# Forming the recurrent row's decays, key directions and deviations in PSUM banks: a two-block transformer kernel on one core

## The reference, cut to what matters

```
w_log = -softplus(-(w0 + tanh(w_low) @ w2)) - 0.5
decay = exp(-exp(w_log))                      # = exp(-exp(-0.5) * sigmoid(w0 + ...))
a = sigmoid(a0 + a_low @ a2)
g = sigmoid(g_low) @ g2
k_mod = k * (1.0 + (a - 1.0) * k_a)
kk = heads(k * k_k)
kk = kk / maximum(sqrt(sum(kk * kk, axis=-1)), 1e-12)
# scan over the positions t, 16 heads of 64 x 64 state
sa = state @ (-kk)
state = state * decay + sa * (kk * a) + v * k_mod
y = state @ r
# behind the scan, for each head
y = (y - mean) * rsqrt(var + 64e-5) * lnx_w + lnx_b
out = (y + sum(r * k_mod * r_k) * v) * g
```

## Time and profile before

| what | value |
|---|---|
| median of 3 runs | 2094.07 us (2093.38 to 2094.23) |
| the profiled execution's own time | 2093.18 us |
| its span | 2091.4 us |
| PE busy | 2035.6 us (97%) |
| PE weight loads busy | 1680.5 us (80%) |
| DVE busy | 1196.7 us (57%) |
| ACT busy | 535.9 us (26%) |
| POOL busy | 1107.7 us (53%) |
| mean granted clock of TensorE | 0.991 |

### The profile page before, as it was taken

One profiled execution on the slowest core, in us unless ns is written; L12 is line 12 of the kernel. 1 busy time (PEld: TensorE's weight loads), 2 busy tenths in 40 slices (PEclk: granted clock), 3 DMA queues, 4 the chain that ended last, 5 costly groups with the idle time before them and its releaser, 6 DMA issues.

```text
span 2091.4 us, 39582 instructions
## 1 busy us (share of the span) xinstructions
PE 2035.6 (97%) x16195; PEld 1680.5 (80%) x16195; DVE 1196.7 (57%) x1533; ACT 535.9 (26%) x1139; POOL 1107.7 (53%) x859
## 2 busy tenths in 40 slices
PE   8999999999999999999997999999999999999998
PEld 6888788878877788788876888888886878888886
DVE  7888724466667664302068676666673756565413
ACT  2100002233434212313142133333223023333101
POOL 6777764634534464454546044423364756666663
PEclk9999999999999999999999999999999999999999
DMA  4333232253443422212322022111213432322231
GB/s 135 101 101 101 92 99 65 90 166 121 141 147 116 136 81 81 81 61 70 115 66 82 14 66 66 36 56 46 65 63 116 140 101 81 100 96 88 92 111 55
DMA packets 181242, 190.27 MB, mean 91 GB/s; under 512 B 8526, under 2 KB 162269, under 8 KB 180829
## 3 DMA queue, kind: packets, MB, share of 16 engines
q1 hardware_dynamic: 172288, 181.81, 27.4%
q10 hardware_dynamic: 8796, 6.21, 1.0%
HBM read 179.56 MB, written 8.44 MB: 90 GB/s over the span
## 4 chain that ended last, share of the span: by engine, by line
PE 60%; DVE 4%; POOL 1%; issue 1%; DVEq 1%; POOLq 1%; ACT 0%; ACTq 0%
PE bank L907 8%; PE bank L909 8%; PE bank L908 8%; PE bank L1584 7%; PE bank L1545 3%; PE bank L1397 3%; PE bank L1413 2%; PE bank L1415 2%; PE bank L1414 2%; PE bank L1682 2%; PE bank L1319 1%; PE bank L1321 1%; PE bank L1320 1%; PE bank L1072 1%; PE bank L1286 1%
## 5 line engine op out<-in xcount | busy, mean ns | idle before, releaser
L738 POOL TENSOR_TENSOR wlo<-raws,whi 128x1024 fp32r<-128x1024 f32 (+5 forms) x312 | 677.6, 2172 | 46.6 <-issue 4.4
L736 POOL TENSOR_SCALAR whi<-raws 128x1024 fp32r<-128x1024 f32 (+5 forms) x312 | 331.9, 1064 | 306.8 <-PE bank L1074 173.0
L907 PE MATMUL bank<-hbuf,whi 128*128 128x512 f32 (+2 forms) x840 | 328.9, 392 | 0.0
L909 PE MATMUL bank<-hbuf,wlo 128*128 128x512 f32 (+2 forms) x840 | 327.7, 390 | 0.0
L908 PE MATMUL bank<-hbuf,whi 128*128 128x512 f32 (+2 forms) x776 | 302.7, 390 | 0.0
L649 POOL TENSOR_TENSOR spare<-ones 1x1 f32<-1x1 f32 x92 | 22.3, 243 | 345.2 <-PE bank L909 243.3
L907 PEld LDWEIGHTS bank<-hbuf,whi 128*128 128x128 f32 (+2 forms) x840 | 157.0, 187 | 35.1 <-POOL wlo L738 1.1
L909 PEld LDWEIGHTS bank<-hbuf,wlo 128*128 128x128 f32 (+2 forms) x840 | 157.0, 187 | 34.4
L908 PEld LDWEIGHTS bank<-hbuf,whi 128*128 128x128 f32 (+2 forms) x776 | 144.9, 187 | 31.1
L672 POOL TENSOR_SCALAR lg2L<-lg 128x128 fp32r<-128x128 f32 x8 | 2.7, 342 | 235.2 <-DMA lg<-in_g 235.2
L2667 DVE TENSOR_REDUCE nmax<-bank 128x4 f32<-128x512 f32 (+3 forms) x40 | 21.1, 550 | 145.5 <-PE bank L1294 104.2
(11 more groups left out here) (542 smaller groups left out, 4730.7 us busy)
## 6 DMA issues: line engine op xcount, KB each, us to landing
adaw<-in_w_ada SPq DMA_DIRECT2D x64, 384.0 KB, 3.9
raws<-in_w_up SPq DMA_DIRECT2D x22, 1024.0 KB, 4.9
raws<-in_w_in SPq DMA_DIRECT2D x41, 512.0 KB, 4.0
raws<-in_w_in SPq DMA_DIRECT2D x18, 1024.0 KB, 5.0
raws<-in_pool_w_in SPq DMA_DIRECT2D x16, 1024.0 KB, 5.4
raws<-in_mla_w_in SPq DMA_DIRECT2D x10, 1024.0 KB, 5.6
raws<-in_pool_w_out SPq DMA_DIRECT2D x8, 1024.0 KB, 5.0
raws<-in_mla_w_out SPq DMA_DIRECT2D x8, 1024.0 KB, 5.3
```

What stands on the lines that cost most here:

```text
L736: G.tensor_scalar(h_, r_, 1.0, 1.0, ALU.mult, ALU.mult)
L738: G.tensor_tensor(l_, r_, f32(h_), ALU.subtract).then_inc(raw_split, 1)
L907: M.matmul(dst, wh, acts[k][0], start=(first and k == 0), stop=False)
L909: mm = M.matmul(dst, wl, acts[k][0], start=False, stop=(last and k == n - 1))
```

## The change

It keeps a set of intermediates in PSUM banks in place of SBUF tiles. For pairs 1 and up the rates and their scanned sums lie in bank 5 (`decay_tiles`), for pairs 2 and up the grown decays too; the lengths, directions and scaled keys of all pairs lie in bank 3; the deviations of pairs 0 to 6 lie in bank 4 (`deviation_tile`). The tile kk and its multiplication are gone (ACT squares Kr with the column as its scale), and so is the multiplication by -exp(-0.5), which moves into the scales of the exponentials. ACT writes one more sigmoid for each of the pairs 1 to 7. `decayed_keys` keeps its eight instructions and gains three drains. The banks stay in use for longer, so PE gets other waits, and the second and third of the three started groups change places. Pair 0 keeps its decays in SBUF, and rT of pairs 0 and 1 still reads two SBUF tiles; so does L2868, which is not touched.

```diff
+        def deviation_tile(p):
+            return bank[4] if p < PAIRS - 1 else gn_dev
+        def decay_tiles(q):
+            return (lwd if q == 0 else bank[5], cc if q == 0 else bank[5], epos if q < 2 else bank[5])
...
             def lora_products(q):
...
                 else:
-                    pe.wait_ge(sem("rk.sig"), q)
+                    pe.wait_ge(sem("rk.kr"), q)
...
             def key_norms(q):
...
-                elif q >= 2:
+                else:
+                    pe.wait_ge(sem("rk.bon"), q)
+                if q >= 2:
                     pe.wait_ge(sem("gn.q"), q - 1)
...
             def chain(p):
...
                 started(2, Gak, vtok).then_inc(sem("sq.r"), 1)
-                pe.wait_ge(sem("rk.nr"), min(p + 2, PAIRS))
-                started(3, vtok, Gqk)
                 if p >= 1:
-                    pe.wait_ge(sem("gn.s"), p)
+                    pe.wait_ge(sem("rk.y"), p + 1)
                 else:
                     pe.wait_ge(sem("gt.taken"), 4)
                 started(4, kN, vtok, hi=CHUNKS - 1)
+                pe.wait_ge(sem("rk.bon"), min(p + 2, PAIRS))
+                started(3, vtok, Gqk)
                 pe.wait_ge(sem("inv.dve"), (p + 1) * TAKEN_ALL)
+                pe.wait_ge(sem("rk.kr"), min(p + 2, PAIRS))
                 pe.wait_ge(sem("rk.sig"), min(p + 2, PAIRS))
...
-                A.activation(lwd[:, :], lora_bank(q)[:, :], ACT.Sigmoid, bias=pc[:, 3:4])
+                rate = A.activation(lwd[:, :], lora_bank(q)[:, :], ACT.Sigmoid, bias=pc[:, 3:4])
+                if q:
+                    rate = A.activation(bank[5][:, :], bank[5][:, :], ACT.Sigmoid, bias=pc[:, 3:4])
+                rate.then_inc(sem("rk.rate"), 1)
...
             def key_squares(q):
-                act.wait_ge(sem("rk.kk"), q + 1)
-                A.activation(tile(sq, 0), kk[:, :], ACT.Square).then_inc(sem("rk.sq"), 1)
+                act.wait_ge(sem("rk.pc"), q + 1)
+                act.wait_ge(evac[1], fill("rkv", 1) + q + 1)
+                A.activation(tile(sq, 0), Kr[:, :], ACT.Square, scale=pcol[q % 3][:, 5:6]).then_inc(sem("rk.sq"), 1)
...
-                V.tensor_scalar(kk[:, :], Kr[:, :], pcol[q % 3][:, 5:6], None, ALU.mult).then_inc(sem("rk.kk"), 1)
...
-                V.tensor_scalar(lwd[:, :], lwd[:, :], -float(np.exp(-0.5)), None, ALU.mult)
...
+            def key_directions(q):
+                lengths = bank[3]
+                dve.wait_ge(sem("rk.nr"), q + 1)
+                V.reciprocal(lengths[:, :], lengths[:, :])
+                dve.drain()
+                V.scalar_tensor_tensor(lengths[:, :], Kr[:, :], pcol[q % 3][:, 5:6], lengths[:, :], ALU.mult, ALU.mult)
+                dve.drain()
+            def decayed_keys(q):
+                pc, par = pcol[q % 3], q % 2
+                direction = change = key = bank[3]
                 dve.wait_ge(sem("rk.sig"), q + 1)
                 dve.wait_ge(sem("rk.ex"), q + 1)
+                V.scalar_tensor_tensor(aT[par][:, :], direction[:, :], -1.0, lwd[:, :], ALU.mult, ALU.mult)
+                dve.drain()
+                V.tensor_tensor(direction[:, :], direction[:, :], cc[:, :], ALU.mult)
+                dve.drain()
+                V.tensor_tensor(bT[:, :], direction[:, :], aa[:, :], ALU.mult).then_inc(sem("rk.ab"), 1)
+                dve.drain()
+                V.tensor_scalar(change[:, :], aa[:, :], pc[:, 6:7], pc[:, 10:11], ALU.mult, ALU.add)
+                dve.drain()
+                V.tensor_tensor(key[:, :], Kr[:, :], change[:, :], ALU.mult)
+                dve.drain()
+                V.scalar_tensor_tensor(kkT[:, :], key[:, :], SCAN_SCALE, cc[:, :], ALU.mult, ALU.mult)
+                V.scalar_tensor_tensor(rT[par][:, :], Rr[:, :], SCAN_SCALE, decay_tiles(q)[2][:, :], ALU.mult, ALU.mult)\
                     .then_inc(sem("rk.kr"), 1)
                 dve.drain()
+                V.scalar_tensor_tensor(Rr[:, :], key[:, :], pc[:, 7:8], Rr[:, :], ALU.mult, ALU.mult)\
                     .then_inc(sem("rk.bon"), 1)
...
             def finished(p):
-                x, pc = gn_x, pcol[p % 3]
+                dev, pc = deviation_tile(p), pcol[p % 3]
                 dve.wait_ge(sem("gn.s"), p + 1)
-                V.reciprocal(gn_dev[:, :], gn_dev[:, :])
+                V.reciprocal(dev[:, :], dev[:, :])
                 dve.drain()
-                V.scalar_tensor_tensor(x[:, :], gn_y[:, :], pc[:, 8:9], gn_dev[:, :], ALU.mult, ALU.mult)
+                V.scalar_tensor_tensor(dev[:, :], gn_y[:, :], pc[:, 8:9], dev[:, :], ALU.mult, ALU.mult)
```

More of the change, by code:

```diff
@@ L34 @@
 SCAN_SCALE = 2.0 ** -20
+DECAY_RATE = float(np.exp(-0.5))
 KEY_MIN = 1e-12
@@ L368, in build @@
                     cc = sb("cc", [P, S], F32, st3)
-                    kk = sb("kk", [P, S], F32, st3)
+                    sb("beside_keys", [P, S], F32, st3)
                     epos = sb("epos", [P, S], F32, st3)
@@ L1530, in mix_part @@
                         pe.wait_ge(sem("gn.s"), PAIRS)
+                        pe.wait_ge(sem("rk.y"), PAIRS)
                     elif (kind, i, half) == ("r", 1, 1):
@@ L1749, in _ @@
                     if n == 3 * DT:
-                        pe.wait_ge(sem("rk.sig"), 2)
+                        pe.wait_ge(sem("rk.ex"), 2)
                     gate_part(1, n)
@@ L2167, in key_squares @@
             def key_squares(q):
-                act.wait_ge(sem("rk.kk"), q + 1)
-                A.activation(tile(sq, 0), kk[:, :], ACT.Square).then_inc(sem("rk.sq"), 1)
+                act.wait_ge(sem("rk.pc"), q + 1)
+                act.wait_ge(evac[1], fill("rkv", 1) + q + 1)
+                A.activation(tile(sq, 0), Kr[:, :], ACT.Square, scale=pcol[q % 3][:, 5:6]).then_inc(sem("rk.sq"), 1)
             def key_lengths(q):
                 act.wait_ge(sem("rk.ss"), q + 1)
-                A.activation(tile(sq, 1), bank[3][:, :], ACT.Relu, bias=key_floor)
+                A.activation(bank[3][:, :], bank[3][:, :], ACT.Relu, bias=key_floor)
@@ L2174, in key_lengths @@
                 act.drain()
-                A.activation(tile(sq, 1), tile(sq, 1), ACT.Sqrt, bias=key_rise).then_inc(sem("rk.nr"), 1)
+                A.activation(bank[3][:, :], bank[3][:, :], ACT.Sqrt, bias=key_rise).then_inc(sem("rk.nr"), 1)
             def decays(q):
+                _, sums, grown = decay_tiles(q)
                 act.wait_ge(sem("rk.lp"), q + 1)
-                A.activation(epos[:, :], cc[:, :], ACT.Exp)
-                A.activation(fade[q % 2][:, 0:CHUNKS - 1], fade[q % 2][:, 0:CHUNKS - 1], ACT.Exp)
@@ L2181, in decays @@
-                A.activation(lwd[:, :], lwd[:, :], ACT.Exp)
-                act.drain()
-                A.activation(cc[:, :], cc[:, :], ACT.Exp, scale=-1.0).then_inc(sem("rk.ex"), 1)
+                A.activation(lwd[:, :], lwd[:, :], ACT.Exp, scale=-DECAY_RATE)
+                A.activation(fade[q % 2][:, 0:CHUNKS - 1], fade[q % 2][:, 0:CHUNKS - 1], ACT.Exp, scale=-DECAY_RATE)
+                if q:
+                    A.activation(cc[:, :], sums[:, :], ACT.Exp, scale=DECAY_RATE)
+                    act.drain()
+                    A.activation(grown[:, :], sums[:, :], ACT.Exp, scale=-DECAY_RATE).then_inc(sem("rk.ex"), 1)
+                else:
+                    A.activation(grown[:, :], sums[:, :], ACT.Exp, scale=-DECAY_RATE)
+                    act.drain()
+                    A.activation(cc[:, :], sums[:, :], ACT.Exp, scale=DECAY_RATE).then_inc(sem("rk.ex"), 1)
@@ L2185, in deviations @@
             def deviations(p):
                 act.wait_ge(sem("gn.v"), p + 1)
-                A.activation(gn_dev[:, :], bank[4][:, :], ACT.Sqrt, scale=1.0 / 64, bias=gneps_c[:, 0:1])\
+                A.activation(deviation_tile(p)[:, :], bank[4][:, :], ACT.Sqrt, scale=1.0 / 64, bias=gneps_c[:, 0:1])\
                     .then_inc(sem("gn.s"), 1)
@@ L2754, in take_key @@
                 take_product(q, 1, Kr)
[L2755 removed]
             def log_decays(q):
[L2759 to L2760 removed]
+                rates, sums, _ = decay_tiles(q)
+                dve.wait_ge(sem("rk.rate"), q + 1)
+                V.tensor_tensor_scan(sums[:, :], restart[:, :], rates[:, :], 0.0, ALU.mult, ALU.add)
                 dve.drain()
[L2762 removed]
+                V.tensor_copy(mid[:, :], sums[:, CH // 2 - 1:S:CH])
                 dve.drain()
[L2764 to L2766 removed]
+                V.tensor_tensor(by_chunk(sums[:, :]), by_chunk(sums[:, :]),
                                 mid[:, :].unsqueeze(2).to_broadcast([P, CHUNKS, CH]), ALU.subtract)
                 dve.drain()
[L2769 to L2770 removed]
+                V.tensor_tensor(fade[q % 2][:, 0:CHUNKS - 1], sums[:, CH - 1:S - CH:CH], mid[:, 1:CHUNKS], ALU.add)
+                V.tensor_tensor(lwd[:, :], sums[:, :], lwd[:, :], ALU.subtract).then_inc(sem("rk.lp"), 1)
             def key_directions(q):
+                lengths = bank[3]
                 dve.wait_ge(sem("rk.nr"), q + 1)
[L2775 removed]
+                V.reciprocal(lengths[:, :], lengths[:, :])
```

(1 more changed line is left out.)

22 lines of the change are left out of this document (3 added, 19 removed).

## The result

Six executions of the changed kernel took 2100.92 to 2104.48 us, median 2102.97; six of the kernel before, taken beside them, 2092.14 to 2094.23, median 2093.18. The ratio is 1.0054 (95% interval 1.0035 to 1.0073): 9.8 us slower. The profiled execution took 2104.48 us over a span of 2102.5; the forecast for it was 2104.7.

A forecast was written before the change was run, and what follows sets the result against it. PE, busy for 97% of the span, was taken to bound the kernel. The terms 5.1 + 0.6 + 3.8 + 2.0 gave +11.5 on 2093.18, so 2104.7 profiled; the forecast time was 2105.0 us, range 2099.5 to 2110.

The forecast's parts named there:

- Term 1: At the start, PE's first low-rank product of pair 1 waits 14.8 us for rk.kr, replacing older waits: net +5.1 us.
- Term 2: Before chain(0), DVE's `decayed_keys(1)` gets longer by drains and slower forms, lengthening PE's wait: +0.6 us.
- Term 3: At the start of chain(7), kN waits for rk.y with Gqk now behind it: +3.8 us, and +2.0 of clock.
- Term 4: In chains 1 to 6, Gqk waits for rk.bon, which comes in time by a margin of 0.6 us: cost 0.
- Rival A: The steady chains wait too, as bank operands take longer: +2.4, up to +5 us, time 2108 to 2111; chance 0.12.
- rival B: Not slower: at the start DVE stops losing to POOL, rk.kr comes earlier; time 2091.8 to 2097.6 us; chance 0.08.

The follow-up runs named there:

- b1_kr: The kernel before with one edit, the first low-rank product of pair 1 waiting for rk.kr of pair 0; 2095.79 us.
- e1_lora: The changed kernel with the first low-rank product of pair 1 waiting for rk.sig of pair 0 again; 2086.24 us.
- a_again: The changed kernel run once more, with no edit; 2100.51 us, ratio 1.0059 to the kernel before.
- e2_last: The changed kernel with the deviations of pair 6 in SBUF and kN of chain(7) waiting for gn.s again; 2097.17 us.
- b2_y: The kernel before with kN of chain(7) waiting for rk.y, Gqk still ahead of kN; 2097.09 us (2087.65 to 2106.53).
- e4_two_more: The changed kernel with kkT of the pairs 2 to 7 formed three times over; 2110.09 us.
- b3_sums: The kernel before with only the rates and scanned sums of pair 1 in bank 5; 2082.27 us, ratio 0.9973.

## Why the prediction was right

*Term 1, the start (+5.1).* Its parts were a wait of 14.8, one of 1.4 and 11.08 taken away; measured 14.86 and 1.39, so +5.2, and the clock's slow stretch came again behind the new wait (6.0 us at 0.50 for 5.8 at 0.51), at a net of 0 as put. b1_kr shows that the wait alone makes 2.7 of the 4.1 us at the start, without the rest of the change; e1_lora, which takes it out again, that it is the cause. The reason given for the 6.69 falling away, that the work on pair 1 follows the matmuls as they finish, leaves out what b1_kr shows: POOL was idle then, and the races were not lost. rT took 0.68 with POOL idle beside it; e1_lora has 2.53 with POOL at work.

*Term 2, before chain(0) (+0.6).* The wait grew by 0.63. But the slow clock behind it, 0.77 over 7.4 us before, did not come: 1.7 us were given back which no step of mine had. That is why the start is longer by 4.1 and not by 5.8. It was chance, not the change: a_again, the same kernel with the same wait of 2.99, was granted 0.77 over the 7.4 us there, and of the twelve executions profiled six were and six were not.

*Term 3, chain(7) (+3.8 and +2.0).* 3.95 and, with the 5.8 of the table's last column, 1.8 of clock. e2_last undoes it for the 5.8 us. The clock part was luckier than it looked: b2_y shows some 9 us for the same kind of wait in one execution.

*Term 4, the steady chains (0, with a margin of 0.6).* The cost was right, +0.2 over six chains, and the margin was not: 0.06 in the profile of the changed kernel, 0.4 by e4_two_more. DVE's row from vT to Rr took 11.7 us for 11.1: 0.43 of issue ahead of bT, 0.15 ahead of aT, and 0.12 on L2814, whose bank costs it more than a plain product's length. Rival A stood much nearer than its chance of 0.12 said; the reason given against it was about right for the plain forms (692 and 700 ns, 750 and 756), and the margin was eaten by issue gaps that the sum had left out.

*The sum.* +11.5 was forecast for the profiled execution, +11.3 came (2104.48 over 2093.18); the medians differ by 9.8, inside the range. That it is so near is partly luck. The 1.7 us of clock given back ahead of chain(0) were nearly balanced by what no term had: the 0.2, 0.6 and 0.4 of the table, 1.2 us in all, and 0.2 by which the own time grew more than the span. And the 11.08 us taken away in term 1 hold the wait of 6.69, which stands in the upper group of the kernel before alone; against an execution of the lower group the same changed kernel is 17 to 22 us slower (2102.97 over 2080.9 to 2085.5).

*What the prediction missed.* I wrote that what the change aims at stands elsewhere than on the path. e1_lora and b3_sums show otherwise: at the start the relief was worth 9 us against the execution shown, and was costed as nothing gained because the wait took it over. My rival B had DVE's lost races in the right part of the program but at pair 0's instructions, where a_again shows 1.1 us by them; the ones that decide are pair 1's scans, and they sometimes fall the other way with no change at all.
